# Stick-breaking attention: the sums over later keys from softplus values in two rounded parts, in place of float32 products

## The reference

```
def stick_breaking(q, k, v, out_g):
    ...
    def block(i, qb):
        q_pos = i * Q_BLOCK + jnp.arange(Q_BLOCK, dtype=jnp.int32)
        z = jnp.einsum('bqhd,bkhd->bhqk', qb, k,
                       preferred_element_type=jnp.float32) * (SB_DIM ** -0.5)
        earlier = k_pos[None, :] < q_pos[:, None]
        log_beta = jax.nn.log_sigmoid(z)
        log_1m_beta = jnp.where(earlier, jax.nn.log_sigmoid(-z), 0.0)
        later = lax.cumsum(log_1m_beta, axis=3, reverse=True) - log_1m_beta
        a = jnp.where(earlier, jnp.exp(log_beta + later), 0.0)
        return jnp.einsum('bhqk,bkhd->bqhd', a.astype(v.dtype), v)
```

## Time and profile before

| | |
|---|---|
| median of 3 runs | 3208.31 us |
| the runs | 3206.8 to 3211.69 us |
| the profiled execution, its span | 3208.3 us |
| busy share PE, PEld, DVE, ACT, POOL | 96%, 75%, 50%, 45%, 23% |
| HBM traffic | 280 MB, 87 GB/s over the span |

### The profile page before, as it was taken

How to read it: one execution, slowest core, us unless ns; L and a number is a source line. 1 busy time by engine, 2 the same in 40 slices (tenths; PEclk the granted TensorE clock), 3 DMA queues, 4 the chain that set the end, 5 groups by cost and what they waited for, 6 DMA issues and landing times.

```text
span 3208.3 us, 43608 instructions
## 1 busy us (share of the span) xinstructions
PE 3068.1 (96%) x13579; PEld 2420.0 (75%) x13579; DVE 1620.1 (50%) x2405; ACT 1437.2 (45%) x2106; POOL 736.4 (23%) x508
## 2 busy tenths in 40 slices
PE   8999999999999999999989989999999998899998
PEld 6888888788887777888867756688877765668887
DVE  6544455575566877565567464411135646441113
ACT  4333334453334775333356664532244666542224
POOL 2333323100000000000022213244442220334444
PEclk9999999999999999999999989999999998899999
DMA  5332322343332232423212112133342220223334
GB/s 159 95 107 87 90 77 77 89 122 99 93 97 79 73 112 73 138 86 104 81 52 60 55 34 66 53 98 93 92 124 54 60 61 21 66 66 94 96 92 131
DMA packets 490391, 273.02 MB, mean 85 GB/s; under 512 B 9551, under 2 KB 479767, under 8 KB 489849
## 3 DMA queue, kind: packets, MB, share of 16 engines
q1 hardware_dynamic: 485576, 264.52, 28.7%
q10 hardware_dynamic: 4656, 6.58, 0.6%
HBM read 267.75 MB, written 12.21 MB: 87 GB/s over the span
## 4 chain that ended last, share of the span: by engine, by line
issue 56%; PE 29%; POOL 11%; DVE 2%; ACT 1%; POOLq 0%; ACTq 0%; DMA 0%; DVEq 0%
PE acc L748 9%; PE acc L749 9%; PE acc L754 8%; POOL s_w_lo L717 5%; POOL s_w_lo L716 5%; PE acc L751 1%; PE wide L775 1%; PE misc L749 0%; PE misc L748 0%; PE misc L754 0%; DVE s_sc L2568 0%; PE wide L748 0%; POOLq L110 0%; PE misc L775 0%; PE wide L749 0%
## 5 line engine op out<-in xcount | busy, mean ns | idle before, releaser
L748 PE MATMUL acc<-s_h_hi,s_w_hi 128*128 128x512 f32 (+1 forms) x1920 | 790.6, 412 | 34.2 <-DVE s_h_lo L2402 13.5
L749 PE MATMUL acc<-s_h_lo,s_w_hi 128*128 128x512 f32 (+1 forms) x1920 | 756.2, 394 | 0.0
L716 POOL TENSOR_TENSOR s_w_lo<-s_raw,s_w_hi 128x512 fp32r<-128x512 f32 x212 | 275.0, 1297 | 2057.7 <-ACT s_w_hi L1590 2056.4
L754 PE MATMUL acc<-s_h_hi,s_w_lo 128*128 128x512 f32 (+1 forms) x1680 | 662.8, 395 | 0.0
L1590 ACT ACTIVATE s_w_hi<-s_raw 128x1024 fp32r<-128x1024 f32 x386 | 409.4, 1061 | 373.1 <-DVE s_x L3245 210.8
L748 PEld LDWEIGHTS acc<-s_h_hi,s_w_hi 128*128 128x128 f32 x1920 | 364.8, 190 | 135.8 <-issue 32.9
L749 PEld LDWEIGHTS acc<-s_h_lo,s_w_hi 128*128 128x128 f32 x1920 | 365.1, 190 | 87.8 <-issue 11.8
L754 PEld LDWEIGHTS acc<-s_h_hi,s_w_lo 128*128 128x128 f32 x1680 | 319.3, 190 | 73.9
L699 POOL TENSOR_TENSOR s_w_lo<-s_raw,s_w_hi 128x1024 fp32r<-128x1024 f32 x80 | 191.6, 2395 | 407.2 <-ACT s_w_hi L1590 405.6
L717 POOL TENSOR_TENSOR s_w_lo<-s_raw,s_w_hi 128x512 fp32r<-128x512 f32 x212 | 278.4, 1313 | 0.0
L748 PE MATMUL acc<-s_hid_hi,s_w_hi 128*128 128x512 f32 x704 | 278.1, 395 | 0.0
(11 more groups left out here) (473 smaller groups left out, 5360.3 us busy)
## 6 DMA issues: line engine op xcount, KB each, us to landing
s_raw<-w_ff SPq DMA_DIRECT2D x128, 512.0 KB, 4.0
s_raw<-ffn_w_up SPq DMA_DIRECT2D x96, 512.0 KB, 3.9
s_raw<-attn_w_qkv SPq DMA_DIRECT2D x72, 512.0 KB, 3.7
s_raw<-ffn_w_down SPq DMA_DIRECT2D x48, 512.0 KB, 3.9
s_raw<-w_in SPq DMA_DIRECT2D x48, 512.0 KB, 4.0
s_raw<-lru_w_in SPq DMA_DIRECT2D x16, 512.0 KB, 4.0
s_raw<-w_out SPq DMA_DIRECT2D x16, 512.0 KB, 4.0
s_bd<-bias_by_head SPq DMA_DIRECT2D x24, 256.0 KB, 4.7
```

What stands on the lines that cost most here:

```text
L716: pool.tensor_tensor(w_lo_b[s][:, 0:h, :], raw_b[s][:, 0:h, :], w_hi_b[s][:, 0:h, :].bitcast(F32), ALU.subtract)
L748: mm(out, ahi, bhi, start=start, stop=False, **kw)
L749: mm(out, ahi, blo, start=False, stop=False, **kw)
L754: mm(out, alo, bhi, start=False, stop=stop, **kw)
```

## The change

The softplus values are split into a rounded high part `l_hi` (ACT, a copy, `softplus_hi`) and a low part `l_lo` (DVE, a subtraction, `softplus_lo`), and each product of `sb_later` becomes two F32R products, of `l_hi` and of `l_lo`, with rounded copies `sums_r` of the two tables. The tables hold only 0 and -1. `l_lo` lies where the softplus values were, `l_hi` in space that the memory's keys take later. PE waits for `l_lo` of each block where it waited for `l_sum`.

ACT makes the copy of block j + 1 behind the three steps of block j, and that of block 0 last; it waits for DVE's `l_sum` of the block. DVE makes `l_lo` of block j + 1 behind its own step on block j. The tables are loaded by a DMA of their own at the start and rounded once on ACT in the first block; an unused table is gone.

```
     def sb_later(zs):
         for j in reversed(range(TT)):
-            pe.wait_ge(sems["l_sum"], count("l_sum"))
+            pe.wait_ge(sems["l_lo"], count("l_lo"))
+            kw = dict(start=False, skip_group_check=True)
             for j2 in reversed(range(j, TT)):
-                args = (zs[j][:, (j2 - j) * P:S - j * P], square[:, LATER if j2 == j else MINUS, :],
-                        sd[:, 0, LSTART[j2]:LSTART[j2 + 1]])
-                kw = dict(start=False, stop=j2 == j, skip_group_check=True)
+                w, o = slice(LSTART[j2], LSTART[j2 + 1]), zs[j][:, (j2 - j) * P:S - j * P]
+                summed = sums_r[:, 0 if j2 == j else 1, :]
+                mm(o, summed, l_hi[:, w], stop=False, **kw)
                 if j2 == j:
-                    mm(*args, **kw).then_inc(sems["z_full"], 1)
+                    mm(o, summed, l_lo[:, w], stop=True, **kw).then_inc(sems["z_full"], 1)
                     count("z_full")
                 else:
-                    mm(*args, **kw)
+                    mm(o, summed, l_lo[:, w], stop=False, **kw)
...
+    def softplus_hi(j):
+        w = slice(LSTART[j], LSTART[j + 1])
+        act.wait_ge(sems["l_sum"], count("l_sum"))
+        fn(l_hi[:, w], sd[:, 0, w], ACT.Copy).then_inc(sems["l_hi"], 1)
+        act.wait_ge(sems["l_hi"], count("l_hi"))
...
     def sb_softplus():
...
             fn(sd[:, 0, w], sd[:, 0, w], ACT.Ln, bias=1.0).then_inc(sems["l_done"], 1)
             act.wait_ge(sems["l_done"], count("l_done"))
+            if j < TT - 1:
+                softplus_hi(j + 1)
+        softplus_hi(0)
...
+    def softplus_lo(j):
+        w = slice(LSTART[j], LSTART[j + 1])
+        dve.wait_ge(sems["l_hi"], count("l_hi"))
+        tt(l_lo[:, w], sd[:, 0, w], l_hi[:, w].bitcast(F32), ALU.subtract).then_inc(sems["l_lo"], 1)
+        count("l_lo")
...
     def sb_softplus():
         for j in reversed(range(TT)):
             w = slice(LSTART[j], LSTART[j + 1])
             dve.wait_ge(sems["l_done"], count("l_done"))
             stt(sd[:, 0, w], next_wide()[:, 0:S - j * P], 0.0, sd[:, 0, w], ALU.max, ALU.add).then_inc(sems["l_sum"], 1)
-            count("l_sum")
+            dve.wait_ge(sems["l_sum"], count("l_sum"))
+            if j < TT - 1:
+                softplus_lo(j + 1)
+        softplus_lo(0)
...
+    def later_sums():
+
+        act.wait_ge(sems["consts_in"], count("consts_in", 64))
+        fn(sums_r[:], sums[:], ACT.Copy).then_inc(sems["sums_ready"], 1)
+        act.wait_ge(sems["sums_ready"], count("sums_ready"))
```

More of the change, by code:

```diff
@@ L221, in shape_constants @@
     later = -(pos[:, None] >= pos[None, :]).astype(np.float32)
-    earlier = (pos[:, None] < pos[None, :]).astype(np.float32)
     forbid = np.where(pos[:, None] < pos[None, :], 0.0, NEG).astype(np.float32)
@@ L225, in shape_constants @@
     chunks[:CHUNK, S - CHUNK:] = NEG
-    square = np.stack([np.eye(P, dtype=np.float32), ones, halves, turn, later, -ones, earlier, forbid], axis=1)
+    square = np.stack([np.eye(P, dtype=np.float32), ones, halves, turn, forbid, later, -ones], axis=1)
     return {"c_hot": hot, "c_hot2": hot2, "c_rope": rope, "c_square": square, "c_chunks": chunks}
@@ L237 @@
 UNITS_LAYER = 4 + len(UNITS_2) + 2 + KC + 2 + 2 + 2 * (D_FF_2 // P)
-IDENT, ONES, HALVES, TURN, LATER, MINUS, EARLIER, FORBID = range(8)
+IDENT, ONES, HALVES, TURN, FORBID, LATER, MINUS = range(7)
+KEPT = FORBID + 1
 def plan_columns():
@@ L271, in build_program @@
             "hi_split unit_ready ffn_ready acc_full acc_freed misc_act misc_dve "
-            "consts_in square_in f_in x_in0 x_in1 params_in zeroed t_done x_ready cols_in f_full f_copied f_stored bias_spread bias_in "
+            "consts_in sums_ready l_hi l_lo square_in f_in x_in0 x_in1 params_in zeroed t_done x_ready cols_in f_full f_copied f_stored bias_spread bias_in "
             "h_hi h_lo sq_ready ss_ready stat_full rstd_ready res_mid "
@@ L300, in build_program @@
         cols = sb("cols", [P, COL_TILES * P])
-        square = sb("square", [P, 8, P])
+        square = sb("square", [P, KEPT, P])
+        sums_r = sb("sums_r", [P, 2, P], F32R)
         eps = sb("eps", [P, 1])
@@ L346, in build_program @@
         f_sb = sb("f_sb", [GROUPS * HEADS, F_W], F32, sub)
+        sums = sb("sums", [P, 2, P], F32, sub)
         hot2 = sb("hot2", [BUCKETS + 1, F2_W], F32, sub)
@@ L403, in build_program @@
         yo = sb("yo", [P, KC, S], F32, stage)
+        part = ExitStack()
+        l_hi = sb("l_hi", [P, TRI[TT]], F32R, part)
+        part.close()
         mk_hi, mk_lo = (sb(n, [P, 2, N_MEM], F32R, stage) for n in ("mk_hi", "mk_lo"))
@@ L418, in build_program @@
         vt2, kr = (sb(n, [P, S], F32, sub) for n in ("vt2", "kr"))
+        part = ExitStack()
+        l_lo = sb("l_lo", [P, TRI[TT]], F32R, part)
+        part.close()
         sd = sb("sd", [P, 2, TRI[TT]], F32, sub)
@@ L541, in constants @@
                 sp.dma_start(f_dram.ap(), f_sb[:]).then_inc(sems["f_stored"], 16)
-                sp.dma_start(square[:, 2:, :], t["c_square"][:, 2:, :]).then_inc(sems["consts_in"], 16)
+                sp.dma_start(square[:, 2:, :], t["c_square"][:, 2:KEPT, :]).then_inc(sems["consts_in"], 16)
+                sp.dma_start(sums[:], t["c_square"][:, LATER:MINUS + 1, :]).then_inc(sems["consts_in"], 16)
                 sp.dma_start(hot2[:], t["c_hot2"]).then_inc(sems["consts_in"], 16)
@@ L818, in second_table @@
             def second_table():
-                pe.wait_ge(sems["consts_in"], count("consts_in", 48))
+                pe.wait_ge(sems["consts_in"], count("consts_in", 64))
                 pe.wait_ge(sems["f_copied"], count("f_copied", 3))
@@ L1561, in _ @@
             count.w = 0
+            pe.wait_ge(sems["sums_ready"], count("sums_ready"))
             with count.loop(LAYERS,
                             "mla_sq acc_freed acc_full h_lo hid_lo hn_lo hn_sq m_lo misc_act misc_dve kr_in o_lo om_full "
-                            "l_sum p_ready po_freed po_full rot_full ss_ready stat_full unit_ready v_turned wide_freed "
+                            "l_lo p_ready po_freed po_full rot_full ss_ready stat_full unit_ready v_turned wide_freed "
                             "wide_full z_full") as i:
@@ L1705, in beside_first @@
                     memory_rstd()
+                    later_sums()
             def head(first):
@@ L2364, in _ @@
                             "mla_sq a_exp acc_freed acc_full exp_done h_hi hi_split hid_hi hid_lo hn_hi hn_norm hn_rstd "
[L2365 removed]
+                            "hn_sq kr_in l_abs l_done l_hi l_sum m_hi misc_act mla_ln mn_in nmax_ready o_hi om_full po_freed pt_hi raw_B0 "
                             "raw_B1 raw_B2 raw_B3 rope_done rstd_ready sq32 sq_ready ss_ready stat_full v_hi v_turned "
@@ L3255, in _ @@
                             "mla_sq a_mid acc_freed acc_full bd_cut bd_in exp_done h_hi h_lo hid_hi hid_lo hn_hi hn_lo hn_norm "
-                            "hn_rstd kr_in l_done l_sum m_hi m_lo misc_dve mla_norm mn_in nmax_ready o_hi o_lo "
+                            "hn_rstd kr_in l_done l_hi l_lo l_sum m_hi m_lo misc_dve mla_norm mn_in nmax_ready o_hi o_lo "
                             "p_ready po_freed po_full pt_hi recip rope_done rot_full rstd_ready sq_ready ss_ready v_hi "
```

1 line of the change is left out of this document (removed).

## The result

| | before | after |
|---|---|---|
| median | 3209.95 us (4 runs) | 3221.84 us (4 runs, 3218.56 to 3225.1) |
| span of the profiled execution | 3208.3 us | 3218.5 us |
| granted clock over the span | 0.976 | 0.971 |

The ratio is 1.0038, 95% interval [1.0026, 1.0051], so +12 us with about 4 to either side. The forecast was 3215.2 us, +6.9. The direction was right. The time lies 0.8 us above the top of the range. ("After" is the changed kernel, "before" the kernel before it.)

The account below looks back on a forecast made before the run. PE, busy for 96% of the span, was taken to bound the kernel. A layer's terms, -0.2 - 1.6 + 4.0 + 1.2 = +3.4 us, gave +6.9 for two layers on 3208.3: 3215.2 us, range 3208 to 3221.

Parts of the forecast that it names:

- The price of the products: In PE's sums, twenty rounded products take 2.74 us a head instead of 4.43, a possible gain of 13 us.
- Pair one: First head keeps only 0.2 of 1.65 us because `al` comes late behind POOL; second head gains 1.6: -1.8 a layer.
- Pair two: PE waits for ACT and DVE: +1.5 at the first head, +4.9 before the memory's keys, +4.0 at latent attention.
- The sum: A layer: -0.2 - 1.6 + 4.0 + 1.2 = +3.4 us, +2.2 without the clock; two layers +6.9 us.
- The clock: The granted clock falls behind the longer wait before pair two's transposes, costing 0.4 to 1.7 us a layer, taken as 1.2.
- The base: The forecast starts from the profiled 3208.3 us of the kernel before, taken to be the median too.
- The clock doesn't fall: Rival: no fall at the longer wait before the transposes, +2.2 us a layer, 3212.7 us; chance 0.22 for 3210 to 3213.5.
- More is lost: Rival: `al` misses POOL's boundary in pair one, or the clock stays low past `memory_kv(0)`: 3218 to 3222 us; chance 0.15.
- The faster rival: Copies fit into idle time and PE sees only shorter sums: -13 us, 3195 us; chance 0.10 for around 3207 or better.

Follow-up runs that it names:

- the filled kernels: The changed kernel with useless 512-column products put into PE's waits; the three with the wait before pair two's transposes filled: ratios 1.0018 to 1.0020.
- the kernel with three waits filled: The changed kernel with 5, 10 and 22 useless products before pair one's second-head score, pair two's transposes and the memory's keys: 3214.87 us, ratio 1.0018.
- the products alone: The kernel before with twenty rounded products a head, both reading the high part, and no added step on ACT or DVE: 3201.26 us, ratio 0.9975.
- DVE making both parts: The changed kernel with nothing added on ACT: DVE makes the rounded high part by a second maximum step, then the low part: 3207.27 us, ratio 0.9994.
- the first pair alone: The change made in the first pair of heads only, the second pair keeping float32 sums and no copies: 3205.87 us, ratio 0.9991.

## Why the prediction had the waits right and the clock too small

- **The price of the products: right.** The ten pairs take 2.76 us in the trace of after (1789.09 to 1791.85; forecast 2.74):

```profile
1789.09 0.22 PE L1286 MATMUL wide<-s_l_hi,s_sums_r 128*128 128x128 f32 x1
...
1791.39 0.39 PE L1286 MATMUL wide<-s_l_hi,s_sums_r 128*128 128x512 f32 x1
1791.62 0.39 PE L1288 MATMUL wide<-s_l_lo,s_sums_r 128*128 128x512 f32 x1
1791.85 0.40 PE L757 MATMUL acc<-s_h_hi,s_w_hi 128*128 128x512 f32 x1
```

  From start to start a rounded product of 128 columns takes 0.11 us where it follows another of 128, as taken. A float32 product is two instructions in the trace: twice 0.11 us at 128 columns and twice 0.43 at 512. Two rounded ones (0.46 us at 512) cost about half of it at 512 and three quarters to all of it at 128. How 128 columns follow a wider product, and each other, can be read in the trace of before:

```profile
1780.98 0.29 PE L754 MATMUL acc<-s_ah,s_vl 128*128 128x256 f32 x1
1781.10 0.22 PE L748 MATMUL acc<-s_ah,s_vh 128*128 128x128 f32 x1
1781.16 0.28 PE L749 MATMUL acc<-s_al,s_vh 128*128 128x128 f32 x1
1781.27 0.27 PE L751 MATMUL acc<-s_ah,s_vl 128*128 128x128 f32 x1
1781.38 0.45 PE L748 MATMUL acc<-s_h_hi,s_w_hi 128*128 128x512 f32 x1
```

  Behind the product of 256 columns the first of 128 is followed by the next after 0.06 us, the other two take 0.11 each. A weight load takes 0.19 us on PEld. Among the products of 512 columns each load starts with the product ahead of its own, 0.23 us before its own; from 1781.11 on the loads start 0.10 to 0.12 us apart, as the narrow products do.
- **Pair one: right.** PE goes on at 1768.80 behind `al`, 0.3 us earlier than before relative to the start of the stage (forecast 0.2), and the second head keeps 1.6 where the clock stays up (the pair ends 1.9 us earlier in layer 1 of after; forecast 1.8). Alone the pair gives -3 us, forecast -3.6. That a step of POOL holds `al` up is in the trace of before (L2972): four times `al` of 128 columns began inside one, took 0.95 to 1.16 us and ended 0.15 us behind the step's end; the four times without one it took 0.29. It changed nothing here: the copy's end at 1767.6 and 0.3 us give the same 1767.9, and in after `al` took 0.37 us.

```profile
1768.38 0.37 DVE L3008 TENSOR_TENSOR s_al<-s_sd,s_ah 128x128 fp32r<-128x128 f32 x1 [0.76 <-ACT s_ah L2138]
...
1768.80 0.32 PE L1271 MATMUL wide<-s_qh,s_kh 64*128 64x128 f32 x1 [1.20 <-DVE s_al L3008]
```

- **Pair two: right.** The wait before the transposes is 3.09 us (3.2 to 3.5 expected; the copies cost 2.15 us there, not 2.47), the one before latent attention 3.21 (3.2 to 3.4), the one before the memory's keys 5.66 where PE isn't late (5.5 to 6). Before the memory's keys PE starts 5.6 us later than before, counted from the end of pair one's second sums (where after stood at +0.5); forecast were 4.9 and some of the clock. Twelve layers of the changed kernel, with waits filled and without, were profiled. Seven grew by 1.7 to 2.0 us over the stage, those in which the low clock lay in waiting time or beside steps that another engine paces (the memory's keys, a chunk every 0.72 us); the other five grew by 4.5 to 6.0. The sum had 2.2 for the waits without the clock.
- **The clock: the step that failed.** The prediction costed one fall a layer, behind the transposes, "taken as 1.2", and its sum has nothing for the clock anywhere else. The fall that it costed was sized well: 1.3 us on average over nine layers. At the memory's keys, where the sum has nothing either, a slow clock cost 0.1 to 0.2 us. The term left out is pair one: the new wait of 1.2 us before its second head was worked out, and no clock was priced at it. In the four profiled layers of after low clock ahead of pair one's second sums cost 1.5, 0, 2.9 and 1.9 us, 1.6 a layer and 3.1 for both (the last of them not behind that wait). In all the four layers grew by 4.1 us on average, 2.3 more than the 1.8 of the layers without such loss, so 4.6 us for both layers; the filled kernels give 6 us, 3.5 to either side. The sum had 2.4. This is 2 to 3.5 us of the miss of 5 in the difference. Which of the two waits the missing part belongs to is open, since filling pair one's alone gave nothing.
- **The base.** The part on the profile before said that nothing of the profiled execution lies outside its span. In all later executions of that kernel the time is 1.7 to 1.9 us more than the span (in two of the filled kernels up to 3.5), so the span of 3208.3 would belong to an execution of 3210.1 us, and the median of before is 3209.3 us over 31 runs, 1 us above the base used. That is 1 to 1.7 us of the absolute miss, and none of the ratio. Twice +3.4 is 6.8, not 6.9, which changes nothing.
- **What stays open.** The waits took 0.8 us less than the sum had, so some 2 to 4 us of the miss remain. In the two profiles of after another +3.9 and -0.8 us lie outside the stage, in work that the change doesn't touch. Of the +3.9, time lost to the low clock makes +4.5 and idle time -0.7. Whether the change moves these or they differ by chance from one execution to the next can't be told from single profiles.
- **The rivals.** "The clock doesn't fall" is what the kernel with three waits filled shows: +5.8 us measured (3 to 9), +4.4 forecast. As an argument against it the prediction said that 3.4 us is longer than any wait that left the clock alone; a wait of 3.09 us did so twice. "More is lost" (3218 to 3222, chance 0.15) is what happened, though not by the causes it named: the clock was low at the start of the memory's keys (1838.4 to 1845.2 in after), but that cost 0.1 us, and filling that wait as well gave nothing more (3214.87 against 3214.62); and `al` in pair one didn't miss a boundary. The faster rival falls with the kernel that has the products alone: even that gives 8, not 13.

## What to carry to other kernels

A cheaper step on the bounding engine can be worth nothing if its preparation is put on the engine for which the bounding one waits (here 1.0038 with the copies on ACT, 0.9994 with DVE making both parts, for the same products): ask first whose queue the preparation goes into and what stands behind it there, and try the engine with slack, even if it needs more steps. When a change makes or lengthens a wait of TensorE, price the clock at every such wait, short ones too (behind the one of 1.2 us it fell in four of eight profiled layers), and look at more than one profile, since two layers or two executions of one kernel differ by microseconds in it. Compare distances between fixed places of the program, which tell what a slow stretch cost; the granted clock alone doesn't: in layer 1 of after slow time from 2606 on, ahead of a wait, cost nothing. When a step is moved behind another, look at everything that is queued behind it, not only at the wait that it was moved for.

## What the runs showed of the hardware

- Useless products in a wait made the kernel faster: 37 a layer, 6 us less than after. In the kernel before 23 a layer gave 2.9 us (0 to 6).
- Stretches at a granted clock of 0.5 were mostly 3.4 or 6.8 us long (345 of 407 in the seventeen traces), costing 1.7 and 3.4 us of full speed where PE had work throughout. Some began without a wait close ahead: with the products alone at 2538.8, 10 us behind the last wait (0.64 us), and with the first pair alone at 2616.5, 11.8 us behind the last wait (0.67 us), where PE is busy throughout:

```profile
2616.00:2623.50 7.50, 7.50 (x24) 5.79 (x24) 3.12 (x6) 6.33 (x14) 0.00 (x0) 0.54 0.00 0
```

- A maximum with a rounded output straight from the bank takes DVE as long as one with a float32 output (0.69 us each for 512 columns, 1825.53 and 1826.26 where DVE makes both parts), so the rounded high part needed no copy of its own on ACT.
- A float32 product of 512 columns took PE 0.86 us and a rounded one 0.23; at 128 columns it was 0.22 and 0.06 to 0.11. So here rounding made wide products nearly four times cheaper, narrow ones two to four times.
